# Two heads' scores at once in the gated memory, decay and gate projections likewise, and new begin times

## What is computed

```python
# gated memory, per head of width 64, tokens t and s <= t
scores = q @ k.T * 64 ** -0.5 * exp(gate weights of t and s)
num    = scores @ [v, 1]               # the last column gives the denominator
h      = num / max(abs(den), exp(-m)) * sigmoid(output gate)
# RWKV: decay and gate of the state from low-rank projections
zw = tanh(u_w) @ w_up                  # 64 -> 256
za = u_a @ a_up                        # 64 -> 256
```

## Time and profile before

| | |
|---|---|
| median of 3 runs | 2409.43 us (2409.38 to 2409.88) |
| profiled execution, own time | 2412.0 us |
| span of its instructions | 2410.7 us |
| TensorE busy | 2363.4 us, 98% |
| VectorE busy | 1515.7 us, 63% |
| ScalarE busy | 1232.0 us, 51% |
| mean granted clock of TensorE | 0.998 |

### The profile page before, as it was taken

The page is one execution under the profiler, slowest core; times in us unless marked ns, Lnnn a source line. Parts: engine busy times, 40 slices in busy tenths (PEclk is TensorE's granted clock), DMA queues, the critical chain, the costliest instruction groups (busy, mean ns, idle before and its releaser), DMA issues.

```text
span 2410.7 us, 31254 instructions
## 1 busy us (share of the span) xinstructions
PE 2363.4 (98%) x12525; PEld 1933.3 (80%) x12525; DVE 1515.7 (63%) x2297; ACT 1232.0 (51%) x2053; POOL 52.5 (2%) x66
## 2 busy tenths in 40 slices
PE   8999999999999999999999999999999999999998
PEld 6788878888888887888878878778877887877886
DVE  5657786655555678665565577775566557676556
ACT  5446554544544655454454464554455446365445
POOL 0000000000000000000000000010000000000000
PEclk9999999999999999999999999999999999999999
DMA  7554445556565544555555542155555554225563
GB/s 249 182 199 149 135 145 184 177 181 196 170 194 182 164 131 140 181 183 187 185 174 185 194 160 83 45 201 188 188 170 175 183 195 137 83 82 180 183 196 123
DMA packets 110738, 399.95 MB, mean 166 GB/s; under 512 B 12289, under 2 KB 12673, under 8 KB 110337
## 3 DMA queue, kind: packets, MB, share of 16 engines
q1 hardware_dynamic: 110592, 397.96, 50.2%
HBM read 396.86 MB, written 1.05 MB: 165 GB/s over the span
## 4 chain that ended last, share of the span: by engine, by line
PE 92%; DVE 6%; ACT 1%; issue 1%; DMA 0%; POOL 0%; SPq 0%; ACTq 0%; DVEq 0%
PE ps L509 80%; PE ps L516 4%; DVE wlo L490 2%; PE ps L2075 1%; PE ps L1481 1%; PE ps L1445 1%; DVE alo L655 1%; PE ps L498 1%; ACT whi L483 1%; PE ps L2453 0%; PE ps L1436 0%; DVE xs L916 0%; PE ps L2428 0%; ACT ahi L636 0%; DVE up L1929 0%
## 5 line engine op out<-in xcount | busy, mean ns | idle before, releaser
L490 DVE TENSOR_TENSOR wlo<-raw,whi 128x1024 fp32r<-128x1024 f32 (+1 forms) x748 | 893.2, 1211 | 294.4 <-ACT whi L483 288.9
L483 ACT CAST whi<-raw 128x1024 fp32r<-128x1024 f32 (+1 forms) x748 | 764.4, 1040 | 346.3 <-PE ps L509 329.6
L509 PE MATMUL ps<-whi,ahi 128*128 128x512 f32 (+2 forms) x2016 | 798.5, 396 | 17.1 <-DVE wlo L490 12.7
L509 PE MATMUL ps<-wlo,ahi 128*128 128x512 f32 (+2 forms) x2016 | 794.5, 394 | 0.0
L509 PE MATMUL ps<-whi,alo 128*128 128x512 f32 (+2 forms) x2016 | 788.1, 391 | 0.0
L509 PEld LDWEIGHTS ps<-whi,ahi 128*128 128x128 f32 x2016 | 379.9, 188 | 108.8 <-DVE wlo L490 26.1
L509 PEld LDWEIGHTS ps<-whi,alo 128*128 128x128 f32 x2016 | 380.0, 189 | 73.9 <-issue 1.7
L509 PEld LDWEIGHTS ps<-wlo,ahi 128*128 128x128 f32 x2016 | 380.1, 189 | 72.4 <-issue 2.6
L509 PE MATMUL ps<-whi,yhi 128*128 128x512 f32 (+1 forms) x948 | 372.4, 393 | 2.6 <-DVE ylo L837 1.4
L509 PE MATMUL ps<-wlo,yhi 128*128 128x512 f32 (+1 forms) x948 | 370.1, 390 | 0.0
L509 PE MATMUL ps<-whi,ylo 128*128 128x512 f32 (+1 forms) x948 | 369.9, 390 | 0.0
(11 more groups left out here) (377 smaller groups left out, 1572.8 us busy)
## 6 DMA issues: line engine op xcount, KB each, us to landing
raw<-stream SPq DMA_DIRECT2D x718, 512.0 KB, 4.0
raw<-stream SPq DMA_DIRECT2D x16, 388.0 KB, 3.1
bcb<-bcs SPq DMA_DIRECT2D x9, 512.0 KB, 6.3
raw<-stream SPq DMA_DIRECT2D x8, 416.0 KB, 3.7
raw<-stream SPq DMA_DIRECT2D x4, 384.0 KB, 3.2
cst<-consts SPq DMA_DIRECT2D x1, 1260.0 KB, 7.6
msc<-misc SPq DMA_DIRECT2D x1, 1160.0 KB, 7.5
xs<-xin SPq DMA_DIRECT2D x2, 512.0 KB, 4.4
```

What stands on the lines that cost most here:

```text
L483: act.do.copy(whi[:, n % NSP, 0:w], raw[:, n % NRAW, 0:w]).then_inc(*rounded(n))
L490: dve.do.tensor_tensor(wlo[:, n % NSP, 0:w], raw[:, n % NRAW, 0:w], whi[:, n % NSP, 0:w].bitcast(F), ALU.subtract).then_inc(*rest(n))
L509: m = pe.do.matmul(o, a, b, start=(first and q == 0), stop=(last and q == n - 1))
```

## The change

Three edits. The memory's scores are issued for heads 0 and 1 together and for heads 2 and 3 together, alternating between the upper and the lower 64 rows of the array; the first pair waits for the silu and for both halves of the output gates, the second for W of head 1. The decay and gate projections alternate in the same way, behind both waits. Waits for banks that stood ahead of a place for warm matmuls stay there only where there are warm matmuls, and otherwise stand at the work itself. And the tables `WARM` and `PLAN` are written anew for every boundary.

```diff
--- before.py
+++ after.py
 WARM = {
-    "ffn1_2>mix2": {"pe_norm": (0, 0, 3, 0), "pe_scores2": (0, 0, 0, 0, 0, 2, 0, 5), "pe_values2": (0, 0, 0, 0, 6, 3, 3, 5)},
-    "ffn2>ffn1": {"pe_norm": (0, 0, 2, 0)},
-    "ffn2_2>ple": {"pe_norm": (0, 0, 0, 2)},
-    "final>ffn1_2": {"pe_norm": (0, 3, 3, 0)},
-    "mix2>ffn2_2": {"pe_norm": (0, 0, 0, 1)},
-    "ple>ffn1_2": {"pe_norm": (3, 6, 0, 0)},
+    "ffn1_2>mix2": {"pe_scores2": (0, 0, 0, 0, 0, 2, 0, 5), "pe_values2": (0, 0, 0, 0, 5, 3, 3, 3)},
+    "ffn2>ffn1": {"pe_norm": (0, 0, 1, 0)},
+    "ffn2_2>ple": {"pe_norm": (0, 0, 0, 1)},
+    "final>ffn1_2": {"pe_norm": (0, 2, 3, 0)},
+    "ple>ffn1_2": {"pe_norm": (2, 4, 0, 0)},
 }
 PLAN = {
     ">ffn1": {
-        "act_square": (-9.64, -9.3, 14.98, 20.36),
+        "act_square": (4.34, 6.36, 11.68, 12.72),
...
     "ffn1_2>mix2": {
-        "act_memory": (140.1, 144.62, 148.84, 150.26, 158.72, 167.74, 170.32, 176.06, 177.8, 183.4),
+        "act_memory": (137.58, 139.34, 139.44, 145.74, 155.76, 169.3, 173.76, 175.92, 181.38, 183.74),
-        "dve_memory": (94.32, 99.04, 99.62, 101.38, 145.8, 162.22, 164.98, 166.72, 166.86, 169.06, 169.06, 169.06,
-            169.06, 173.48, 178.08, 178.24, 181.66, 182.44, 186.64),
+        "dve_memory": (93.54, 95.3, 103.64, 112.26, 146.66, 154.3, 154.56, 156.04, 159.18, 160.44, 160.84, 161.68,
+            161.68, 165, 173.74, 177.3, 177.34, 178.22, 183.54),
-        "dve_sums2": (149.52, 151.34, 172.2, 172.94),
+        "dve_sums2": (148.98, 151.7, 160.78, 161.4),
-        "pe_memory": (138.8, 147.52, 154.3, 159.02, 162.74, 168.98, 171.42, 171.42, 172.48, 174.5, 177.7, 178.04,
-            182.76),
+        "pe_memory": (137.56, 152.78, 153.26, 158.94, 158.94, 162.52, 165.28, 170.16, 175.7, 176.4, 181.94),
-        "pe_norm": (11.8, 16.82, 19.98, 22.12, 23.48, 23.48, 23.74, 24.44),
+        "pe_norm": (-34.04, 16.4, 21.64, 22.04, 23.12, 24.74, 24.96, 24.96),
...
-        "pe_turn2": (174.76, 174.76),
+        "pe_turn2": (172.96, 172.96),
-        "pe_values2": (104.76, 127.82, 128.4, 128.4, 128.68, 133.04, 137.78, 138.36, 141.58, 142.46, 142.6, 145.84,
-            147.4, 151.88, 159.9, 168.3, 168.3, 170.62, 171.32, 171.32, 172.44, 173.48, 173.74, 173.74),
+        "pe_values2": (126.02, 127.22, 128.06, 128.08, 128.1, 137.38, 137.38, 137.62, 145.56, 147.12, 147.12,
+            148.84, 148.84, 154.78, 157.36, 160.22, 161.24, 161.24, 161.24, 165, 166.94, 168.62, 168.62, 168.84),
...
@@ -490,10 +487,13 @@
             dve.do.tensor_tensor(wlo[:, n % NSP, 0:w], raw[:, n % NRAW, 0:w], whi[:, n % NSP, 0:w].bitcast(F),
                                  ALU.subtract).then_inc(*rest(n))
 
+    def warmth(s, lane, n):
+        counts = WARM.get(boundary(s), {}).get(lane, ())
+        return counts[n] if n < len(counts) else 0
+
     def rewarm(s, lane, n, bank):
 
-        counts = WARM.get(boundary(s), {}).get(lane, ())
-        for _ in range(counts[n] if n < len(counts) else 0):
+        for _ in range(warmth(s, lane, n)):
             pe.wait_ge(warm_dve, "made")
             pe.do.matmul(ps[:, bank, :].rearrange("p (k n) -> p k n", k=4), warm[:, :],
                          warm[:, :].unsqueeze(1).broadcast_to([128, 4, 128]), start=True, stop=True)
@@ -612,10 +612,12 @@
         for i in range(2):
             for hf in range(2):
                 yield turn_time(s, i, hf) - 0.01
-                wait_banks(s, i, hf)
-                rewarm(s, "pe_norm", 2 * i + hf, 2 * i + hf)
+                if warmth(s, "pe_norm", 2 * i + hf):
+                    wait_banks(s, i, hf)
+                    rewarm(s, "pe_norm", 2 * i + hf, 2 * i + hf)
                 yield turn_time(s, i, hf)
                 wait_x(pe, s, i, hf)
+                wait_banks(s, i, hf)
                 m = turns(*((ps[:, 2 * i + hf, 128 * c:128 * c + 128],
                                            xs[:, i, 512 * hf + 128 * c:512 * hf + 128 * c + 128]) for c in range(4)))
                 m.then_inc(*turned(s, i, hf))
@@ -1947,15 +1949,14 @@
         a, gu = MISC["lora", l], MISC["g_up", l]
         yield t + 16.6
         pe.wait_ge(front_act, s, "th")
-        for c in range(2):
-            m = pe.do.matmul(ps[:, 2, 256 * c:256 * c + 256], msc[0:64, a + 128 * c:a + 128 * c + 128], th[0:64, :],
-                             start=True, stop=True)
-        m.then_inc(*front_pe(s, "zw"))
         pe.wait_ge(front_dve, s, "rw", 2)
         for c in range(2):
-            m = pe.do.matmul(ps[:, 3, 256 * c:256 * c + 256], msc[64:128, a + 128 * c:a + 128 * c + 128],
-                             up[64:128, 6, :], start=True, stop=True, tile_position=(64, 0))
-        m.then_inc(*front_pe(s, "za"))
+            mw = pe.do.matmul(ps[:, 2, 256 * c:256 * c + 256], msc[0:64, a + 128 * c:a + 128 * c + 128], th[0:64, :],
+                              start=True, stop=True, tile_position=(0, 0))
+            ma = pe.do.matmul(ps[:, 3, 256 * c:256 * c + 256], msc[64:128, a + 128 * c:a + 128 * c + 128],
+                              up[64:128, 6, :], start=True, stop=True, tile_position=(64, 0))
+        mw.then_inc(*front_pe(s, "zw"))
+        ma.then_inc(*front_pe(s, "za"))
         yield t + 17.4
         pe.wait_ge(front_act, s, "sg")
         for c in range(2):
@@ -2416,13 +2417,18 @@
         for n, i, j, t in JOBS2:
             yield org(s) + 20 + t - 0.01
             k = 128 * (i + 1)
-            if n:
-                pe.wait_ge(job_dve, s, n - 1, "mask")
-            else:
-                pe.wait_ge(front_act, s, "qT")
-                pe.wait_ge(front_dve, s, "qT", 2)
-            rewarm(s, "pe_scores2", n, 5)
+
+            def banks_free():
+                if n:
+                    pe.wait_ge(job_dve, s, n - 1, "mask")
+                else:
+                    pe.wait_ge(front_act, s, "qT")
+                    pe.wait_ge(front_dve, s, "qT", 2)
+            if warmth(s, "pe_scores2", n):
+                banks_free()
+                rewarm(s, "pe_scores2", n, 5)
             yield org(s) + 20 + t
+            banks_free()
             for q in range(2):
                 p = slice(64 * q, 64 * q + 64)
                 m = pe.do.matmul(ps[:, 5 + q, 0:k], qkT[p, j, 128 * i:128 * i + 128], qkT[p, 4, 0:k], start=True,
@@ -2433,13 +2439,18 @@
         for n, i, j, t in JOBS2:
             yield org(s) + 20 + t + 2.99
             k = 128 * (i + 1)
-            if n:
-                pe.wait_ge(job_act, s, n - 1, "back")
-            else:
-                pe.wait_ge(lstm_dve, s, "mq")
-            rewarm(s, "pe_values2", n, 7)
+
+            def bank_free():
+                if n:
+                    pe.wait_ge(job_act, s, n - 1, "back")
+                else:
+                    pe.wait_ge(lstm_dve, s, "mq")
+            if warmth(s, "pe_values2", n):
+                bank_free()
+                rewarm(s, "pe_values2", n, 7)
             yield org(s) + 20 + t + 3.0
             pe.wait_ge(job_act, s, n, "exp", 1)
+            bank_free()
             m = turns(*((ps[:, 7, 128 * q:128 * q + 128], S2[:, n % 2, 128 * q:128 * q + 128])
                                       for q in range(2 * (i + 1))))
             m.then_inc(*job_pe(s, n, "turn"))
@@ -2551,27 +2562,30 @@
                 o = 8 * q + 4 * i
                 m = pe.do.transpose(ps[:, 3, o:o + 4], src[:, 128 * i:128 * i + 128], ident[0:4, 0:4])
         m.then_inc(*lstm_pe(s, "cols"))
-        for h in range(4):
-            c, p = h // 2, slice(64 * (h % 2), 64 * (h % 2) + 64)
-            yield t + H2 + 2.2 * h
-            if h == 0:
-                pe.wait_ge(rec_dve, s, "var")
-            elif h == 1:
-                pe.wait_ge(lstm_dve, s, "cols")
+        for c in range(2):
+            for h in (2 * c, 2 * c + 1):
+                yield t + H2 + 2.2 * h
+                if h == 0:
+                    pe.wait_ge(rec_dve, s, "var")
+                elif h == 1:
+                    pe.wait_ge(lstm_dve, s, "cols")
+                else:
+                    pe.wait_ge(lstm_dve, s, "w1", h - 2)
+                pe.do.matmul(ps[:, 2 + h % 2, 0:256], cc("sel")[0:4, 128 * h:128 * h + 128], M_, start=True,
+                             stop=True).then_inc(*lstm_pe(s, "sel", h))
+            yield t + H2 + 4.4 * c + 2.6
+            if c == 0:
+                pe.wait_ge(lstm_act, s, "silu")
+                pe.wait_ge(lstm_act, s, "og", 1)
             else:
-                pe.wait_ge(lstm_dve, s, "w1", h - 2)
-            pe.do.matmul(ps[:, 2 + h % 2, 0:256], cc("sel")[0:4, 128 * h:128 * h + 128], M_, start=True,
-                         stop=True).then_inc(*lstm_pe(s, "sel", h))
-            yield t + H2 + 2.2 * h + 0.4
-            if h < 2:
-                pe.wait_ge(lstm_act, s, "silu")
-                pe.wait_ge(lstm_act, s, "og", h)
-            else:
-                pe.wait_ge(lstm_dve, s, "W", h - 2)
-            pe.do.matmul(ps[:, h % 2, 0:256], cv[p, 2 + c, 0:128], cv[p, c, :], start=True, stop=True,
```

(75 more changed lines are left out.)

207 lines of the change are left out of this document (76 added, 131 removed), and 61 rows, old and new, of the table PLAN.

## The result

The changed kernel takes 2424.77 us in the median of 4 runs (2417.86 to 2427.60), the kernel before 2409.65 us in runs of the same kind (2409.38 to 2410.60). The medians differ by 15.1 us, and the profiled executions by 12.1 us (2424.13 against 2412.0). The ratio on record is 1.0049, interval 1.0038 to 1.0061, so 9 to 15 us: slower, where 4 us faster had been forecast, and above the whole range. The wide spread goes with TensorE's mean granted clock, 0.995 in the run of 2417.86 us and 0.991 in that of 2427.60.

The account below looks back on a forecast made before the run. TensorE, busy 98% as a queue of matmuls, was taken as the bound. Terms A to G sum to −4.15 us, taking 2412.0 to 2407.85 us, a median of 2405.3 us; 8-in-10 range 2398 to 2413 us.

Parts of the forecast that it names:

- the rival that has one: Clock rival: falls at openings without warm matmuls, 1.4 us each, seven to be slower; chance 0.03 inside the bounds, 0.02 slower.
- A: Tail of mix2: memory scores of two heads at once take 1.08 us a pair, saving 2.5 us.
- VectorE keeps the tail: Rival for the tail of mix2: VectorE stays the limit, pairs are worth nothing, 2407.8 us; chance 0.06.
- B: Decay and gate projections: eight records in 1.30 instead of 1.35 us, saving 0.1 us for both layers.
- C: Warm matmuls: 21 fewer, only those in front of ready work count, saving 1.5 us.
- D: Tail of mix2: head 3's chain falls behind the attention's output, delaying the memory's sums 1.5 us a layer, +3.0 us.
- E: Opening of mix2: a ready product moves ahead of a turn into TensorE's 2.15 us hole, −0.9 us.
- F: Start of the kernel: both ScalarE squares precede the first weight rounding, delaying the first product, +0.85 us.
- G: All other begin times at every boundary: half of E's share applied to 38.4 us of holes, −3.0 us.
- the slower rival: New order loses in the mixing stages, needing G at +6.0 to exceed 2414.3 us; chance 0.12.

Follow-up runs that it names:

- experiment 7: Paired scores with tables and warm matmuls of the kernel before, second pair ahead of the last values: 2417.61 us, ratio 1.0022.
- experiment 10: As experiment 7, plus seven warm matmuls a layer as filler in TensorE's waits around the last values: 2411.42 us, ratio 0.9997.
- experiment 11: Kernel before without the five warm matmuls ahead of the last transposes, no pairs: 2418.79 us, ratio 1.0028.
- experiment 12: Changed kernel plus ten warm matmuls a layer as filler in the tail of mix2: 2418.92 us, ratio 1.0042.
- experiment 8: Kernel before with only the alternating decay and gate projections: 2412.48 us, ratio 0.9998.
- experiment 2: Changed kernel with the 77 warm matmuls of the kernel before: 2424.38 us, ratio 1.0057.
- experiment 4: Changed kernel with scores 2 and 3 ahead of the last transposes and head 3's chain ahead of the attention's output: 2423.67 us, ratio 1.0061.
- experiment 6: Kernel of experiment 1 with the new begin times only where mix1 and the ffn2 behind it open: 2424.16 us, ratio 1.0046.
- experiment 9: Changed kernel with each head's scores issued singly instead of in pairs: 2433.30 us, ratio 1.0089.
- 1: New code with pairs, but begin times and warm matmuls of the kernel before, second pair behind the last values: 2420.04 us, ratio 1.0040.
- experiment 13: As experiment 10, with one instead of five warm matmuls before the last transposes: 2410.70 us, ratio 0.9994.

## Why the prediction was wrong

**The step that failed first is the clock.** The sum has no term for it, and the rival that has one read one stretch at 0.66 at an opening, priced a fall at 1.4 us, and looked for more of them at openings. They came in the tails instead, and they were longer. By experiments 7 and 10 a fall of 10.2 us costs 4.4 us in the first layer (173.1 against 168.7) and 3.0 in the second; but the second mix2 of 10 has a stretch of 3.4 us at its opening that 7 has not, worth 1.4 us by the earlier trace rows, so it is 4.4 us there as well. By 11, whose falls are 13.6 us, it is 4.6 and 3.3 us although 1.3 us of matmuls had gone from each, so 5.9 us in the first layer, and 6.0 in the second once the opening is counted. All of these are some 0.4 us lost for each us at half clock, an estimate from these differences. The rival's 1.4 us for 3.4 us is the same: its price was right, and the place and the length were wrong. The changed kernel's 20.4 us cost at least 7.1 (176.3 against 169.2 in experiment 12). Two or three of these, not seven, are enough to be slower by the bound. The Trainium skill, "TensorE: Matmul & The Clock Gate", Part 1, "What's actually happening", has TensorE's clock follow how busy it has been; the traces agree in direction, with 12.10 of 14.35 us listed busy before the fall in experiment 7 and 13.21 of 13.94 before the same place in experiment 10, where it held (the line below), and only in part, since it fell after 12.28 of 12.90 in experiment 11:

```profile
1547.56:1561.50 13.94, 13.21 (x83) 10.13 (x83) 10.62 (x23) 10.28 (x27) 0.00 (x0) 1.00 0.01 1
```

**A, −2.5 us: worth 0.** The pair runs at twice the speed (0.85 us for two heads, 1.70 for two single ones), better than the 1.08 us that I took from the attention's rows. The Trainium skill, "TensorEngine Tiling (Array Packing)", "Theoretical Speedup", gives up to 2× for a contraction of 64 rows or less, and the trace agrees. What failed is the count of that time as path. Heads 1 and 3 had stood in waits, for ScalarE's copy behind job 5's transposes (0.68 us) and for the attention's output (0.85 us); with the scores gone the waits show. By experiment 10 the work saved is worth nothing on the path. The rival "VectorE keeps the tail" had the same number, and part of the mechanism: the 0.85 us wait is VectorE's, the 0.68 ScalarE's.

**B, −0.1 us: right within what can be told.** The records fell to 1.06 us, more than I took, and the wait for both halves gave it back (0.55 us in the changed kernel, 0.32 in experiment 8).

**C, −1.5 us: not won.** The 56 records are there. That the five stood in front of ready work was right: experiment 11 starts the last values 1.25 us earlier. But they hold the clock for the rest of the tail, and taking all five costs 7.4 us in two layers. What the two cost that the change takes no run shows by itself: experiment 2 gives all 21 back and stays at 2424.38 us, so in the new order they are worth nothing either way, and the counts alone don't make the changed kernel's loss.

**D, +3.0 us: the mechanism was right**, head 3's chain behind the attention's output and TensorE idle in front of the sums with W as the releaser, 1.38 us in the second layer as forecast. In the first it is 0.57 us, at half clock, where the longer matmuls hide the rest. What the term is worth is not shown: experiment 4 removes the wait and gains nothing, but another of 0.85 us opens in its place.

**E, −0.9 us: right in kind.** A product now stands ahead of the third turn, with 0.94 and 0.75 us of waits about it for the 2.15 of the earlier trace rows:

```profile
1422.71 0.50 PE L509 MATMUL ps<-whi,ahi 128*128 128x512 f32 x1 [0.94 <-DVE wlo L487]
...
1424.20 0.66 PE L516 MATMUL ps<-cst,xs 128*128 128x128 f32 x4 [0.75 <-DVE xs L918]
```

The remainder of the weight wasn't ready, against what I wrote. The stretch at 0.66 in the second opening is gone, though its three warm matmuls are too.

**F, +0.85 us:** the first product starts at 13.44 us for 12.87, +0.57. Mis-sized a little.

```profile
13.44 0.79 PE L509 MATMUL ps<-whi,ahi 128*128 128x512 f32 x1 [3.15 <-DVE wlo L487]
```

**G, −3.0 us: wrong in sign.** Mix1's tables cost some +3 us in two stages (experiment 6), and the other stages outside of the mixers sum up to −0.2, with F's +0.6 in it. The +3 us are half of what the slower rival needed, in two of its four stages; the clock did the rest. Its reason, that a queue 99.6% busy leaves no room for loss, was the reason against it in my text, and the loss came mostly inside busy time. The working of the term was off as well: it takes 0.45 us as a sixth of a hole of 2.85 us, where the earlier trace rows show 2.15 us, so even its own rule would not have given −3.0.

The chances don't fit one another either: 0.14 was given to a time above 2414.3 us, and only 0.1 to one above 2413. The time came out there.

What stays open: which lanes of mix1's tables lose 1.5 us a stage; why experiment 9 is slower than the changed kernel; what in the tables makes the +1.0 us in ple and the −1.0 us in the second ffn1, which experiments 2 and 12 show too, and 1 does not; and how much of the falls in the changed kernel is from fewer matmuls and how much from the waits between them, since one brings the other.

## What to carry to other kernels

Where an engine that is busy 98% has a tail of small matmuls with waits between, making a matmul faster can leave only a longer wait behind it; first look whether what you shorten stands in front of ready work or inside a wait. Price warm matmuls by taking some away on the chip: 0.25 us saved each was here 0.7 us lost each. Look at the granted clock by stretch, since the mean of 0.992 hid 34 us at half clock. If something must be taken out of such a tail, put filler into the waits that it opens, take out only what stands before ready work, as in experiment 13, and look at every run's clock: in experiment 12 two runs of five had the low mean of the changed kernel all the same.
